# Expert gate and up weights loaded in 8192-byte runs, with the gather's columns in the same order

## What is computed

```
def hierarchical_moe(h, router_group, router_expert, w_gate, w_up, w_down):
    # top-1 group of four, then top-2 of the four experts in it
    ...
    y = jnp.zeros_like(h)
    for e in range(N_EXPERTS):
        hid = jax.nn.silu(h @ w_gate[e]) * (h @ w_up[e])
        y = y + combine[..., e:e + 1] * (hid @ w_down[e])
    return y
...
        h = rmsnorm(x, norm_ffn[l])
        x = x + hierarchical_moe(h, router_group[l], router_expert[l], w_gate[l], w_up[l], w_down[l])
```

## Time and profile before

| | |
|---|---|
| median of 3 runs | 3169.62 us |
| profiled execution, its own time | 3166.09 us |
| its span, first to last instruction | 3164.3 us |
| mean granted TensorE clock | 0.977 |
| PE busy | 2975.3 us (94%) |
| PE weight loads busy | 2592.6 us (82%) |
| DVE busy | 1923.8 us (61%) |
| ACT busy | 1635.7 us (52%) |
| DMA | 629.31 MB, mean 199 GB/s |
| weight queue (q1) | 57.5% of 16 engines' span |

### The profile page before, as it was taken

How to read it: one execution, slowest core, us unless ns; L and a number is a source line. 1 busy time by engine, 2 the same in 40 slices (tenths; PEclk the granted TensorE clock), 3 DMA queues, 4 the chain that set the end, 5 groups by cost and what they waited for, 6 DMA issues and landing times.

```text
span 3164.3 us, 41302 instructions
## 1 busy us (share of the span) xinstructions
PE 2975.3 (94%) x16783; PEld 2592.6 (82%) x16783; DVE 1923.8 (61%) x2200; ACT 1635.7 (52%) x1942; POOL 175.2 (6%) x111
## 2 busy tenths in 40 slices
PE   4799999998979999999699999999989999999998
PEld 3798998897867777777599998888869999888886
DVE  3558644533468787888556675555545758555554
ACT  3354444433457777767555644444445554445443
POOL 0403100000000000000000100000000110000000
PEclk8899999999989999999899999999989999999999
DMA  4454557543649898989554555555545545555553
GB/s 150 142 165 147 204 189 243 201 149 120 201 154 352 286 345 284 336 291 360 180 167 160 173 187 186 173 176 183 180 138 190 172 149 194 179 185 173 174 186 133
DMA packets 322887, 629.31 MB, mean 199 GB/s; under 512 B 18425, under 2 KB 28178, under 8 KB 321298
## 3 DMA queue, kind: packets, MB, share of 16 engines
q1 hardware_dynamic: 319776, 617.03, 57.5%
q10 hardware_dynamic: 2642, 8.67, 0.7%
q0 software_dynamic: 288, 1.05, 0.1%
HBM read 619.36 MB, written 7.34 MB: 198 GB/s over the span
## 4 chain that ended last, share of the span: by engine, by line
PE 72%; DVE 10%; ACT 7%; issue 5%; DMA 5%; ACTq 0%; POOL 0%; DVEq 0%; SPq 0%; POOLq 0%
PE pairs L597 14%; PE pairs L599 14%; PE pairs L598 14%; PE pairs L607 8%; PE pairs L609 7%; PE pairs L611 7%; DVE w_lo L1739 5%; ACT w_hi L1240 2%; DMA raw<-in_w_gate_dram 2%; PE misc L985 2%; DMA raw<-in_w_up_dram 2%; PE misc L883 1%; PE misc L720 1%; PE misc L927 1%; ACT scratch L1574 1%
## 5 line engine op out<-in xcount | busy, mean ns | idle before, releaser
L1739 DVE TENSOR_TENSOR w_lo<-raw,w_hi 128x1024 fp32r<-128x1024 f32 x1136 | 1405.7, 1259 | 937.8 <-ACT w_hi L1240 930.8
L1240 ACT ACTIVATE w_hi<-raw 128x1024 fp32r<-128x1024 f32 x1136 | 1178.1, 1058 | 979.6 <-PE pairs L599 581.4
L597 PE MATMUL pairs<-w_hi,a_hi 128*128 128x512 f32 x1664 | 663.5, 399 | 27.5 <-DVE w_lo L1739 22.8
L599 PE MATMUL pairs<-w_hi,a_lo 128*128 128x512 f32 x1664 | 651.6, 392 | 0.0
L598 PE MATMUL pairs<-w_lo,a_hi 128*128 128x512 f32 x1664 | 651.6, 392 | 0.0
L607 PE MATMUL pairs<-a_hi,w_hi 128*128 128x256 f32 x1920 | 557.4, 290 | 47.6 <-DVE w_lo L1739 47.6
L609 PE MATMUL pairs<-a_lo,w_hi 128*128 128x256 f32 x1920 | 549.0, 286 | 0.0
L611 PE MATMUL pairs<-a_hi,w_lo 128*128 128x256 f32 x1920 | 548.5, 286 | 0.0
L607 PEld LDWEIGHTS pairs<-a_hi,w_hi 128*128 128x128 f32 x1920 | 373.8, 195 | 55.1 <-issue 31.4
L597 PEld LDWEIGHTS pairs<-w_hi,a_hi 128*128 128x128 f32 x1664 | 314.4, 189 | 111.8 <-DVE w_lo L1739 33.6
L609 PEld LDWEIGHTS pairs<-a_lo,w_hi 128*128 128x128 f32 x1920 | 374.3, 195 | 0.4
(11 more groups left out here) (312 smaller groups left out, 2315.5 us busy)
## 6 DMA issues: line engine op xcount, KB each, us to landing
raw<-in_w_in_dram SPq DMA_DIRECT2D x232, 1024.0 KB, 5.1
raw<-in_w_out_dram SPq DMA_DIRECT2D x80, 1024.0 KB, 5.0
raw<-in_w_gate_dram SPq DMA_DIRECT2D x64, 1024.0 KB, 7.2
raw<-in_w_up_dram SPq DMA_DIRECT2D x64, 1024.0 KB, 7.3
raw<-in_w_down_dram SPq DMA_DIRECT2D x64, 1024.0 KB, 6.1
raw<-in_xattn_wk_dram SPq DMA_DIRECT2D x16, 1024.0 KB, 5.0
raw<-in_xattn_wv_dram SPq DMA_DIRECT2D x16, 1024.0 KB, 5.0
raw<-in_xattn_wq_dram SPq DMA_DIRECT2D x16, 1024.0 KB, 5.1
```

The costliest lines, as they stand in the source:

```text
L597: nc.tensor.matmul(o, hi[:, k, tok], w_hi[:, s, q, :], start=k == 0, stop=False)
L599: m = nc.tensor.matmul(o, lo[:, k, tok], w_hi[:, s, q, :], start=False, stop=last)
L1240: a.activation(w_hi[:, i % HSLOTS], raw[:, i // 2, 2 * (i % 2):2 * (i % 2) + 2, :], ACT.Copy).then_inc(hi_done, 1)
L1739: v.tensor_tensor(w_lo[:, i % HSLOTS], raw[:, i // 2, 2 * (i % 2):2 * (i % 2) + 2, :], w_hi[:, i % HSLOTS].bitcast(F32), ALU.subtract).the ...
```

## The change

`w_gate` and `w_up` are seen as `(p c)`: partition p holds rows 16 p to 16 p + 15. A chunk still takes four of a partition's sixteen rows, which are now neighbours in memory, 4 x 2048 bytes. k-step j of a product then contracts over rows j, 16 + j, 32 + j, ..., so the gather takes the columns of `x` in steps of 16, and the gain is laid out the same way by a small load of its own, `ffn_gain`. A gather now reads columns of every part of `x`, so it waits for the sums of `x` that stand before it in the order, and it runs after half 7 instead of 6; the copies on ACT and DVE move one half later. The down weights keep their view.

```diff
+        ffn_gain = tiny(KT)
...
-        w_gate, w_up, w_down = (t[n][0].rearrange("e (c p) n -> p e c n", p=P)
-                                for n in ("w_gate", "w_up", "w_down"))
+        w_gate, w_up = (t[n][0].rearrange("e (p c) n -> p e c n", p=P) for n in ("w_gate", "w_up"))
+        w_down = t["w_down"][0].rearrange("e (c p) n -> p e c n", p=P)
...
             sp.dma_start(w_rt[:, :, 4:20], rowview(t["router_expert"][0])).then_inc(rt_in, 16)
+            sp.dma_start(ffn_gain, t["norm_ffn"][0].rearrange("(p k) -> p k", p=P)).then_inc(rt_in, 16)
             sp.dma_start(gain_b, t["norm_final"].rearrange("(a d) -> a d", a=1)
...
+                x_by_row = x[:].rearrange("p t (f k) -> p t k f", k=KT)
+
                 def gather(g, c):
 
                     pe.wait_ge(pick_ok, g + 1)
+                    if g and 4 * (g - 1) + c:
+                        pe.wait_ge(x_added, 4 * (g - 1) + c)
...
-                            m = nc.tensor.matmul(o, x[:, T, c * COLS + k * P:c * COLS + (k + 1) * P],
+                            m = nc.tensor.matmul(o, x_by_row[:, T, 4 * c + k, :],
                                                  pick[:, T, 0:tiles * P], start=T == 0, stop=T == TT - 1)
...
-                            hooks[6] = lambda: gather(g + 1, n)
+                            hooks[7] = lambda: gather(g + 1, n)
...
-                    act.wait_ge(rt_in, 32)
+                    act.wait_ge(rt_in, 48)
...
-                                     ACT.Identity, scale=col("norm_ffn", 4 * c + k))
+                                     ACT.Identity, scale=ffn_gain[:, 4 * c + k:4 * c + k + 1])
...
-                            run(2); gathered_hi(g, 3); run(1); y_copy(g - 1, 3); run(5)
+                            run(3); gathered_hi(g, 3); y_copy(g - 1, 3); run(5)
...
-                        run(2)
+                        run(3)
                         if g < GROUPS - 1:
                             gathered_hi(g + 1, n - 1)
-                        run(1); y_copy(g, n - 1); run(5)
+                        y_copy(g, n - 1); run(5)
...
-                        col("norm_ffn", 4 * c + k), a_hi[:, 4 * c + k, :].bitcast(F32), ALU.mult,
+                        ffn_gain[:, 4 * c + k:4 * c + k + 1], a_hi[:, 4 * c + k, :].bitcast(F32), ALU.mult,
...
-                            run(3); gathered_lo(g, 3); run(4); add_spread(g - 1, 3); run(1)
+                            run(4); gathered_lo(g, 3); run(3); add_spread(g - 1, 3); run(1)
...
-                        run(3)
+                        run(4)
                         if g < GROUPS - 1:
                             gathered_lo(g + 1, n - 1)
-                        run(4); add_spread(g, n - 1); run(1)
+                        run(3); add_spread(g, n - 1); run(1)
```

## The result

| | before | changed |
|---|---|---|
| median | 3167.96 us (7 runs, 3160.65 to 3172.79) | 3179.31 us (7 runs, 3175.30 to 3182.08) |
| profiled execution | 3166.09 us, span 3164.3 | 3180.07 us, span 3178.3 |

The ratio is 1.0038 [1.0029, 1.0048]: slower by 0.4%, 11.4 us. The forecast was 3163.5. The sign is wrong. The time lies outside the forecast's own 3158 to 3169, and inside the wide range only because that took in the rivals. The nearest of their times is the third one's 3177, by luck: its mechanism did not run. The first rival's 3192 had the mechanism.

A forecast was written before the change was run, and what follows sets the result against it. DMA was taken as the longest term in the expert stretch, PE next, 4% below. Packets -8.7, order +1.5 and gain load +0.7 gave -6.5; 3169.62 - 6.5 = 3163.1, stated as 3163.5 us, own range 3158 to 3169, wide range 3157 to 3193.

The forecast's parts named there:

- the wide range: Whole kernel: 3157 to 3193 us, taking in the forecast, the second and third rival and the strided loads.
- the third one's 3177: Late gather costs a real wait at half 3 or 7, 1.2 us more in twelve units, +14: 3177; chance 0.05.
- The first rival: Gather's strided weight loads at half rate: +29 - 6.5 = +22.5, 3192 us; chance 0.27.
- The gather's weight load: Gather on PE, stationary now every 16th column of x: taken as 0, between no cost and +29 us.
- The high bound: Gather's weight load: each pass doubled, 0.11 to 0.22 us, +1.8 us a gather, +29 over 16 gathers.
- Packets, -8.7: Gate and up loads in runs of 8192 bytes: chunk from 2.98 to 2.53 us, stretch 100.3 us, -8.7 us.
- the 4 us of waits that I left for VectorE: Spread-to-gather stretch: PE's 96 us plus 4 us of waits, DVE being busy 88%, taken as 100.3 us.
- the sum of -5: Total change if small-packet overhead follows the skill page, 0.10 us a chunk, with DMA level with PE at 97 us.
- Order, +1.5: Gather behind half 7, copies one half later: -0.5 to +1.5 us a group, taken as +1.5 in all.
- The gain's load, +0.7: New small load behind the router's weights, lengthening ACT's wait: 0 to +3.2 us, taken as +0.7.
- The other three rivals: ACT's DMA waits were covered, 3172 (0.13); late gather really waits, 3177 (0.05); PE's floor reached, 3150 (0.03).

The follow-up runs named there:

- e5_step_and_order: The changed kernel with gate and up weights loaded as before, in runs of 2048 bytes: 3189.18 us, ratio 1.0075.
- e2_order_only: The kernel before with only the new order (gather after half 7, its wait, copies one half later): 3165.82 us, ratio 0.9999.
- e3: The kernel before with only the runs of 8192 bytes for gate and up weights; values and rows do not match: 3155.09 us, ratio 0.9963.
- v5_turned_copy: Kernel before with 8192-byte runs in blocks of 512 rows; gather reads, side by side, GpSimd's copy of x in the weights' order: 3157.12 us, ratio 0.9969.
- v7_turned_early_gain: v5_turned_copy with its gain loaded at the kernel's start on ScalarE's queue: 3155.42 us, ratio 0.9966.
- v2_step_two: Kernel before with two neighbouring rows to a partition, runs of 4096 bytes, gather taking every second column: 3165.44 us, ratio 0.9995.

## Why the prediction was wrong

**The step that failed** is "The gather's weight load … I take 0, nearest to the transpose's row: the same data, the same engine". The runs show +1.59 us a gather in its place (1.80 to 3.40 us; 0.11 to 0.21 a pass) for fourteen of the sixteen gathers and nothing for the first two, 22.3 us in all, and 22.5 by e5_step_and_order. The high bound was +1.8 us a gather, so nearly all of it came. Its ground, that everything doubles at half clock, does not hold for this load: it takes 310 ns at a granted clock of 0.50 and 311 at 1.00. The row that I took was the same data on the same engine, but read side by side; it says how fast such columns are read, and nothing about a step. "No PE row of the trace reads that way" was the truth of it, and then neither end is nearer. What should have decided stands in the prediction's first rival: load and matmul of a gather are level, so nothing hides a longer load, and by its own reckoning a quarter of the high bound was enough to undo the gain.

The rule weighed there (the Trainium skill, Advanced Engine Details and Errata, "SBUF Cachelines") is borne out, and it says more than the prediction used: at least two hits in a 16-byte line are needed to hide the memory's latency. The trace agrees: two hits in each line 196 ns, one hit 311 to 335 ns, one or two hits 261 ns, all at a granted clock of 1.00.

**Packets, -8.7: right, measured -10.7.** Two sizes inside it were off and partly cancelled. A chunk went from 2.98 to 2.78 us of the queues, not to 2.53: the rate was taken from a window of 4.5 us with reads of x, which did not hold for the weights; why was not tried. Yet the stretch fell to 98.3 us, not to 100.3: the 4 us of waits that I left for VectorE were too many. By the estimate from the Trainium skill, DMA: Bandwidth & Descriptors, "Why small descriptors are slow", a chunk would have lost 0.10 us; the 0.20 measured lies between that and the 0.45 read from rows, and the sum of -5 by that estimate is half of the 10.7 measured.

**Order, +1.5: measured 0.0** (e2_order_only). The chain worked out in halves gave a unit of 15.6 to 16.0; it is 15.68. The new wait cost nothing, as said.

**The gain's load, +0.7: at most 0.3 in the trace** (9.48 instead of 9.21 us of idle time).

The parts add up: -10.7 (e3) + 22.5 (e5, step with order and gain) = +11.8; measured +11.4. The first rival had the mechanism. Its +22.5 was 11 us too high: 3.6 because a pass grew by 0.10 and not 0.11 us (25.4 for 29), 2.9 because the first two gathers cost nothing (half by the clock, half because TensorE had stood behind them anyway), and 4.2 because the rest gave -10.7 and not -6.5. The other three rivals are out: the packets did gain, the late gather did not wait, and with the packets alone TensorE still waits 45.5 us for VectorE.

## What to carry to other kernels

A load's order can be made cheap by taking another operand in a new order, but that order is then paid at every read: count the reads and ask what each becomes, and where no row shows such a read, take the unfavourable end unless something hides it. Here 224 of 256 passes at +0.10 us outweighed 128 loads at -0.20 us of queue time. If the layout is worth it, pay for it once on an idle engine: four GpSimd copies of 11 us in all, off the path, turned +11 us into -10 (v5_turned_copy) to -12 (v7_turned_early_gain).

## What the runs showed of the hardware

TensorE's load of 128 fp32 columns by the step between them, the median of the gather's rows, and the 16 passes in the chain. The values of the table are those at a granted clock of 1.00:

| step | 16-byte stretches touched | weight load | 16 passes |
|---|---|---|---|
| 1 (4 bytes) | 32 | 192 ns | 1.80 us |
| 2 (8) | 64 | 196 | 1.89 |
| 3 (12) | 96 | 261 | 2.74 |
| 4 (16) | 128 | 329 | 3.62 |
| 6 (24) | 128 | 317 | 3.47 |
| 8 (32) | 128 | 335 | 3.70 |
| 16 (64) | 128 | 311 | 3.40 |

From 64 stretches to 128 the time follows their number, 65 to 68 ns for 32 more; from a step of 16 bytes on the distance matters little, and 64 bytes is even the quickest of the four. At a granted clock of 0.50 the order turns round: step 1 takes 333 ns, step 4 takes 330 and step 16 310, these two as at full clock. That I had not expected, nor that runs of 4096 bytes moved the queue at 371 GB/s of its own time (14.61 MB at 98.5% of 40 us in v2_step_two), nearly the 377 of 8192, without a gain in the medians. A gain vector in 1024 packets of 8 bytes landed 4.28 us after its issue (v2_step_two), in 128 packets of 64 bytes 3.08 (the changed kernel).
